# Two tiles gathered ahead, one sweep of four dense tiles, and a subtraction on GpSimd, in a hybrid attention and expert-retrieval layer

## The reference

```python
q = (xb @ w_q).reshape(nb, PEER_HEADS, 2, PEER_KEY_DIM // 2)
s1 = jnp.einsum('nhd,hkd->nhk', q[:, :, 0], keys1).astype(jnp.float32)
s2 = jnp.einsum('nhd,hkd->nhk', q[:, :, 1], keys2).astype(jnp.float32)
v1, i1 = lax.top_k(s1, PEER_TOPK)
v2, i2 = lax.top_k(s2, PEER_TOPK)
...
sc, sel = lax.top_k(cand, PEER_TOPK)
idx = jnp.take_along_axis(cidx, sel, axis=-1)
g = jax.nn.softmax(sc, axis=-1)
h = jnp.einsum('nd,nhkd->nhk', xb, u[idx]).astype(jnp.float32)
a = (jax.nn.gelu(h) * g).astype(xb.dtype)
return jnp.einsum('nhk,nhkd->nd', a, v[idx])
```

## Time and profile before

| | us |
|---|---|
| median of 3 runs | 4570.38 (4570.34 to 4610.2) |
| the profiled execution, its own time | 4569.48 |
| its span | 4567.7 |
| stages ahead of the experts | 0 to 2378 |
| experts, from the first dense matmuls to the last | 2403 to 4535 |
| TensorE busy in the span | 4049.8 (89%) |
| VectorE busy in the span | 2861.7 (63%) |
| GpSimd busy in the span | 979.8 (21%) |

### The profile page before, as it was taken

The page is one execution under the profiler, slowest core; times in us unless marked ns, Lnnn a source line. Parts: engine busy times, 40 slices in busy tenths (PEclk is TensorE's granted clock), DMA queues, the critical chain, the costliest instruction groups (busy, mean ns, idle before and its releaser), DMA issues. The chain is left out here.

```text
span 4567.7 us, 60721 instructions
## 1 busy us (share of the span) xinstructions
PE 4049.8 (89%) x19923; PEld 3409.7 (75%) x19923; DVE 2861.7 (63%) x5530; ACT 1447.8 (32%) x2567; POOL 979.8 (21%) x811
## 2 busy tenths in 40 slices
PE   6999798978878756878559999999999999999996
PEld 5788566734456655777548999999999999999996
DVE  4300354311122098888858888888888888888886
ACT  3111233311112113544443333333333333333333
POOL 0000000000000000000004444444444444444441
PEclk9999899789989777888779999999999999999998
DMA  4322421120040100122129999999999999999995
GB/s 142 116 87 79 117 70 42 41 110 28 19 166 0 42 3 11 78 106 124 78 116 378 341 340 340 339 340 339 340 339 340 339 340 339 339 339 341 336 340 212
DMA packets 387884, 905.89 MB, mean 198 GB/s; under 512 B 41664, under 2 KB 185024, under 8 KB 386496
## 3 DMA queue, kind: packets, MB, share of 16 engines
q1 hardware_dynamic: 257696, 491.80, 30.1%
q0 software_dynamic: 110656, 403.62, 25.1%
q10 hardware_dynamic: 19440, 9.44, 0.7%
HBM read 815.62 MB, written 90.18 MB: 198 GB/s over the span
## 5 line engine op out<-in xcount | busy, mean ns | idle before, releaser
L1968 POOL DMA_INDIRECT exp_gu<-in_peer_u_rows,exp_gidx x384 | 487.0, 1268 | 1372.7 <-DMA exp_ggate<-s_ggate 828.9
L2099 PE MATMUL exp_h<-exp_xh,exp_uh 128*128 128x384 f32 x2048 | 688.1, 336 | 47.5 <-DVE exp_ul L2020 47.5
L2101 PE MATMUL exp_h<-exp_xh,exp_ul 128*128 128x384 f32 x2048 | 688.4, 336 | 0.0
L2100 PE MATMUL exp_h<-exp_xl,exp_uh 128*128 128x384 f32 x2048 | 687.1, 335 | 0.0
L2112 PE MATMUL exp_y<-exp_vh,exp_al 128*128 128x512 f32 x1536 | 602.7, 392 | 0.0
L1974 POOL DMA_INDIRECT exp_gv<-in_peer_v,exp_gidx x384 | 473.0, 1232 | 602.4 <-DVE H L2035 520.0
L2111 PE MATMUL exp_y<-exp_vl,exp_ah 128*128 128x512 f32 x1536 | 602.1, 392 | 0.0
L2110 PE MATMUL exp_y<-exp_vh,exp_ah 128*128 128x512 f32 x1536 | 597.2, 389 | 0.0
L1987 ACT ACTIVATE exp_gel<-exp_h 128x384 f32<-128x384 f32 x256 | 126.0, 492 | 1372.7 <-PE exp_h L2101 1372.7
L2035 DVE SCALAR_TENSOR_TENSOR H<-exp_gv,exp_coef,H 128x1024 f32<-128x1024 f32 x384 | 470.6, 1281 | 10.0 <-issue 0.4
L2025 DVE CUSTOM_DVE_ANT_0 exp_gu<-exp_gu,exp_xg 128x1024 f32<-128x1024 f32 x384 | 449.6, 1222 | 0.0
(11 more groups left out here) (293 smaller groups left out, 5982.8 us busy)
## 6 DMA issues: line engine op xcount, KB each, us to landing
exp_u<-in_peer_u SPq DMA_DIRECT2D x256, 512.0 KB, 5.9
exp_v<-in_peer_v SPq DMA_DIRECT2D x256, 512.0 KB, 6.2
exp_w<-s_w SPq DMA_DIRECT2D x256, 192.0 KB, 6.4
...
exp_gu<-in_peer_u_rows,exp_gidx POOLq DMA_INDIRECT x384, 6.3
```

Source lines behind the costliest of these rows:

```text
L1968: pool.indirect_dma_start(out=gu[i % 2][t][:, :], out_offset=None, in_=I["peer_u_rows"], in_offset=bass.IndirectOffsetOnAxis(ap=gidx[:, t, ...
L2099: pe.matmul(hp[s][:, 0:TC], uh[s][:, c, :], xh[k][:, c, :], start=(c == 0), stop=False)
L2100: pe.matmul(hp[s][:, 0:TC], uh[s][:, c, :], xl[k][:, c, :], start=False, stop=False)
L2101: last = pe.matmul(hp[s][:, 0:TC], ul[s][:, c, :], xh[k][:, c, :], start=False, stop=(c == KD - 1))
```

## The change

Tiles 0 and 1 (NE = 2) go through project, diff, window, merge, memory and retrieve alone first; their lists stay in SBUF. The other seven tiles go through the same phases after them. Meanwhile GpSimd fetches the expert rows of the two early tiles (`fetch`), one `u` row per token, tile and list entry (256 units) and then one `v` row, into a ring of slots, and VectorE takes 256 `dot`s and 256 `axpy`s at written places between the phase's own instructions: 140 dots in project, 84 in diff, 32 in window; 24 axpys in window, 124 in merge, 108 in memory. The ring is the seven late tiles of `H` itself, which project reads first and merge reads again from DRAM; in merge and memory it has slots of its own. All loops over tiles are written out. Retrieve of the late tiles makes three gathered and four dense tiles (before: three and six), and `right` has its two last dimensions exchanged.

Experts is one sweep over 128 blocks with four dense tiles (512 columns). h has one PSUM bank, six banks hold the sums of three tiles, and the eighth bank, `spare`, takes the fourth tile's two halves in turn, which VectorE adds to `H` in every block (`add_half`). The three gathered tiles get one list entry per block. vl is subtracted by GpSimd, behind the six gathers of the next block's rows. Of the diff, the helpers, the build and the experts:

```diff
+def fetch(pool, K, table, ring, came, used, units):
+    for j, u in enumerate(units):
+        if j >= len(ring):
+            pool.wait_ge(used, j - len(ring) + 1)
+        pool.indirect_dma_start(out=ring[j % len(ring)], out_offset=None, in_=table,
+                                in_offset=bass.IndirectOffsetOnAxis(ap=K["gidx"][:, u % NE, u // NE:u // NE + 1], axis=0))\
+            .then_inc(came[j % len(ring)], 16)
+def dot(dve, K, ring, came, used, units, j):
+    u, row = units[j], ring[j % len(ring)]
+    dve.wait_ge(came[j % len(ring)], 16 * (j // len(ring) + 1))
+    dve.tensor_tensor_reduce(out=row, in0=row, in1=K["xg"][:, u % NE, :], scale=1.0, scalar=0.0, op0=ALU.mult, op1=ALU.add,
+                             accum_out=K["dots"][:, u % NE, u // NE:u // NE + 1]).then_inc(used, 1)
+def axpy(dve, K, ring, came, used, units, j):
+    u, row = units[j], ring[j % len(ring)]
+    if u % NE == 0:
+        dve.drain()
+    dve.wait_ge(came[j % len(ring)], 16 * (j // len(ring) + 1))
+    dve.scalar_tensor_tensor(out=K["H"][:, u % NE, :], in0=row, scalar=K["dots"][:, u % NE, u // NE:u // NE + 1],
+                             in1=K["H"][:, u % NE, :], op0=ALU.mult, op1=ALU.add).then_inc(used, 1)
...
+DOTS = (140, 84, 32)
+AXPYS = (24, 124, 108)
+MERGE_SLOTS, MEMORY_SLOTS = 7, 3
...
+        dots, axpys = spans(DOTS), spans(AXPYS)
+        early, late = (0, NE), (NE, NT - NE)
...
+            K["ring"] = []
+            phase_project(nc, sem, K, I, S, *early)
+            release()
             with ExitStack() as scope:
-                for name, shape in kept.items():
-                    K[name] = scope.enter_context(nc.sbuf_tensor(name, shape, F32))
-                for phase in phases:
-                    phase(nc, sem, K, I, S)
-            if held:
-                nc.all_engine_barrier()
-                nc.clear_and_free_semaphores(held)
-                nc.all_engine_barrier()
-                held.clear()
+                mixers(scope, 0, NE)
+                phase_diff(nc, sem, K, I, S, *early)
+                phase_window(nc, sem, K, I, S, *early)
+                phase_merge(nc, sem, K, I, S, *early)
+            release()
+            phase_memory(nc, sem, K, I, S, *early)
+            phase_retrieve(nc, sem, K, I, S, *early, NE)
+            release()
+
+            K["ring"] = [K["H"][:, t, :] for t in range(NE, NT)]
+            phase_project(nc, sem, K, I, S, *late, dots[0])
+            release()
+            with ExitStack() as scope:
+                mixers(scope, 1, NT - NE)
+                phase_diff(nc, sem, K, I, S, *late, dots[1])
+                phase_window(nc, sem, K, I, S, *late, dots[2], axpys[0])
+                phase_merge(nc, sem, K, I, S, *late, axpys[1], MERGE_SLOTS)
+            release()
+            phase_memory(nc, sem, K, I, S, *late, axpys[2], MEMORY_SLOTS)
+            release()
+        phase_retrieve(nc, sem, K, I, S, *late, NG)
+        release()
+        phase_experts(nc, sem, K, I, S)
+        phase_final(nc, sem, K, I, S)
...
                                 last = pe.matmul(kp[2 * r + n // 4][:, (n % 4) * P:(n % 4 + 1) * P], left[r][:, n, :],
-                                                 right[r][:, :, n], start=True, stop=True)
+                                                 right[r][:, n, :], start=True, stop=True)
...
-SWEEPS = 2
-SD = ND // SWEEPS
-TC = SD * P
-NY = 2 * SD
-NQ = SWEEPS * NKEY
+TC = ND * P
+NY = 2 * (ND - 1)
+FIRST_G, FIRST_D = NE, NE + NG
...
-                pool.wait_ge(lists_in, 32)
-                pool.wait_ge(xg_ready, NG)
-                for i in range(NKEY):
+                def up(i):
...
+                def low_v(q):
+                    pool.wait_ge(vh_ready, q + 1)
+                    pool.tensor_tensor(vl[q % 2][:, :], v[q % 2][:, :], vh[q % 2][:, :], ALU.subtract).then_inc(vl_ready, 1)
+
+                pool.wait_ge(lists_in, 32)
+                pool.wait_ge(xg_ready, NG)
+                up(0)
+                for i in range(1, NKEY):
+                    up(i)
+                    down(i - 1)
+                    low_v(i - 1)
+                down(NKEY - 1)
+                low_v(NKEY - 1)
...
+                def add_half(q, half):
+                    dve.wait_ge(half_ready, q * 2 + half + 1)
+                    dst = H[:, NT - 1, half * CW:(half + 1) * CW]
+                    dve.tensor_tensor(dst, dst, spare[:, :], ALU.add).then_inc(half_added, 1)
...
+                def step(q, s, turn, turn_before, further=True, first=False):
 
                     dve.drain()
                     dve.wait_ge(w_in[s], 16 * (turn + 1))
                     dve.wait_ge(h_taken, q + 1)
                     dve.tensor_tensor(prod[:, :], gel[:, :], w[s][:, :], ALU.mult).then_inc(p_ready, 1)
-                    dve.wait_ge(vh_ready, q + 1)
-                    dve.tensor_tensor(vl[s][:, :], v[s][:, :], vh[s][:, :], ALU.subtract).then_inc(vl_ready, 1)
                     dve.wait_ge(ah_ready, q + 1)
                     dve.tensor_tensor(al[s][:, :], prod[:, :], ah[s][:, :], ALU.subtract).then_inc(al_ready, 1)
+                    if not first:
+                        add_half(q - 1, 1)
                     if further:
                         low_u(q + 2, s)
-
-                def pair(q, i, x, turn_q, turn_i, further=True, between=None):
-
-                    step(q, 0, turn_q, further)
-                    if between is not None:
-                        add_up(between)
-                    dot(i, x, turn_i)
-                    step(q + 1, 1, turn_q, further)
-                    axpy(i, x, turn_i)
+                    dot(s, turn, 0)
+                    dot(s, turn, 1)
+                    add_half(q, 0)
+                    dot(s, turn, 2)
+                    if not first:
+                        axpy(q - 1, 1 - s, turn_before)
...
+                def product(y, s, t, half, opens, closes):
+
+                    rows, cols = slice(t * P, (t + 1) * P), slice(half * CW, (half + 1) * CW)
+                    pe.matmul(y[:, :], ah[s][:, rows], vh[s][:, cols], start=opens, stop=False)
+                    pe.matmul(y[:, :], ah[s][:, rows], vl[s][:, cols], start=False, stop=False)
+                    return pe.matmul(y[:, :], al[s][:, rows], vh[s][:, cols], start=False, stop=closes)
 
                 def output(q, s, opens=False, closes=False):
                     pe.wait_ge(vl_ready, q + 1)
                     pe.wait_ge(al_ready, q + 1)
+                    if not opens:
+                        pe.wait_ge(half_added, q * 2)
+                    product(spare, s, ND - 1, 0, True, True).then_inc(half_ready, 1)
                     for x in range(NY):
-                        rows, cols = slice(x // 2 * P, (x // 2 + 1) * P), slice(x % 2 * CW, (x % 2 + 1) * CW)
-                        y = yp[x][:, :]
-                        pe.matmul(y, ah[s][:, rows], vh[s][:, cols], start=opens, stop=False)
-                        pe.matmul(y, ah[s][:, rows], vl[s][:, cols], start=False, stop=False)
-                        last = pe.matmul(y, al[s][:, rows], vh[s][:, cols], start=False, stop=closes)
-                    last.then_inc(block_done, 1)
+                        product(yp[x], s, x // 2, x % 2, opens, closes)
+                    pe.wait_ge(half_added, q * 2 + 1)
+                    product(spare, s, ND - 1, 1, True, True).then_inc(half_ready, 1)
+                    pe.sem_inc(block_done, 1)
...
+                with pe.Fori(1, NKEY // 2) as i:
+                    hidden(i * 2, 0)
+                    output(i * 2 - 1, 1)
+                    hidden(i * 2 + 1, 1)
+                    output(i * 2, 0)
+                output(NKEY - 1, 1, closes=True)
```

More of the change, by code:

```diff
@@ new lines, in _ @@
+                high_w(1, 1)
+                for k in range(max(0, n - 4), n - 2):
+                    store_turned(k)
+                for g_ in range(n, total + 2):
+                    c, t = g_ // n, g_ % n
+                    for half in range(2):
+                        if c < CHUNKS - 1 and HIGH_AT[n][half] == t:
+                            high_w(c + 1, half)
+                    if ROPED <= c < ROPED + PLAIN:
+                        plain_rows(g_)
+                    if g_ - 2 < ROPED * n:
+                        store_turned(g_ - 2)
+                    elif g_ - 2 >= (ROPED + PLAIN) * n:
+                        store_turned(g_ - 2 - PLAIN * n)
@@ L363, in project @@
+                        pe.matmul(z[:, 0:width], xh[:, k, at], high, start=(k == 0), stop=False)
+                        pe.matmul(z[:, 0:width], xh[:, k, at], low, start=False, stop=False)
+                        last = pe.matmul(z[:, 0:width], xl[:, k, at], high, start=False, stop=(k == KD - 1))
                     last.then_inc(z_ready, 1)
                 turn_x(0)
-                pe.wait_ge(wl_ready, 2)
-                for t in range(NT):
-                    if t < NT - 1:
-                        turn_x(t + 1)
-                    pe.wait_ge(xl_ready, t + 1)
```

(38 more changed lines are left out.)

1666 lines of the change are left out of this document (864 added, 802 removed).

## The result

The changed kernel takes 4554.38 us in the median of eleven runs (4544.2 to 4562.56); the kernel before, in the eleven runs made beside it, 4602.33 (4565.89 to 4610.2). The ratio is 0.9916, interval [0.9888, 0.9944]: a gain of 0.8%, where 4360 us, 4.6%, was forecast. Of the eleven runs of the kernel before, four lie between 4566 and 4570 and seven between 4601 and 4610; the forecast was built on one of the four, against which the gain is 0.3%. The profiled execution of the changed kernel is its fastest run, 4544.2, with a span of 4542.2 us.

A forecast was written before the change was run, and what follows sets the result against it. TensorE alone was taken to bound the experts, 8.33 us a block. 4569.48 − 350 (experts) + 135 (stages ahead) + 7 (barriers) = 4361, given as 4360; own range 4270 to 4460, with rivals 4190 to 4500.

The forecast's parts named there:

- About 1.8 of 2.5 us ... is added to VectorE: Experts: engines take turns, so about 1.8 us of GpSimd's 2.5 us subtraction lengthens VectorE's block, 11.96 to 13.8 us.
- I take 0.4 of it, 12 a tile, −47: Retrieve: the new layout of right speeds matmuls, 29 us a dense tile; 0.4 kept, 47 us saved over four tiles.
- The exposed rows: Late stages: of 614 us of early tiles' dots and axpys on VectorE, 158 us lengthen the stages.
- my own bound, 96: Late diff stage: 84 dots, 96 us, don't fit VectorE's idle pieces; exposed between 0 and 96, 60 taken.
- VectorE's sum of a block: Experts: VectorE's work per block with vl gone, summed by instruction starts, 11.96 us before any loss to GpSimd.
- The slow rival: Experts: subtraction takes 4.8 us, all taken from VectorE; block 16.75 us, total 4737; chance 0.10.
- the point where the change stops paying: Experts: break-even at 15.4 us a block, a loss of 3.5 us a block to GpSimd.
- the low rival (no turns): Experts: VectorE stays at 11.96, GpSimd's 12.5 us or the DMA bounds the block; total 4195; chance 0.22.
- Rival 3: Late stages don't hide the early tiles' rows: 350 of 614 us exposed instead of 158; total 4550; chance 0.12.
- that dot kept its 1.23: Experts, for no turns: a VectorE dot kept its length while GpSimd's gather issue beside it stretched from 0.94 to 1.68.

The follow-up runs named there:

- the fill: Changed kernel with GpSimd filling vl with zeros (memset, no read) instead of subtracting, same place in its queue: 4196.47 us in two runs.
- the copy: Changed kernel with GpSimd copying v into vl (one operand read) instead of subtracting, at the same place: 4378.78 us in two runs.
- the move in the queue: Changed kernel with GpSimd's subtraction of vl put ahead of its three gathers of v rows instead of behind them: 4467.9 us, ratio 0.9754.
- the kernel before with this one part: Kernel before with only vl's subtraction moved from VectorE to GpSimd, between its gathers: 4875.18 us, ratio 1.0619.
- the dots better placed: Changed kernel with vl back on VectorE and 54 of diff's 84 dots moved to project (30) and window (24): 4176.08 us, ratio 0.9106.

## Why the prediction was wrong

The forecast was 4360 and the time 4554, 194 us more. The way was right: TensorE is no longer the bound, VectorE is, and what GpSimd's subtraction does to VectorE decides. Three terms were too small or did not come.

- **"About 1.8 of 2.5 us ... is added to VectorE" failed.** 2.75 is added. The rest was meant to lie in VectorE's wait for ah or beside the additions that read PSUM; the rows show the subtraction starting 0.49 us after that wait is over, and al then ends 0.57 us after it. VectorE itself sets this place: its first dot of a block frees the buffer that GpSimd waits for (3511.65), the six gathers are issued without another wait, and the subtraction stands behind them (3520.34), so it meets al in 120 of 128 blocks. The block is 14.7 and not 13.8: 0.9 × 128 = 115 us. That the two engines take turns is shown by the fill (nothing lost), the copy (1.40 for 1.05), the move in the queue and the kernel before with this one part. "SBUF — State Buffer", section "Who interferes with whom", of the Trainium skill says that a VectorE instruction with two SBUF inputs contends with a GpSimd instruction that reads SBUF; these runs agree, with VectorE the loser for 2.14 to 2.75 us and GpSimd for 0.86. On who loses, that the first to start keeps the port, they agree only in part: the dot that began 0.23 us ahead of the subtraction was left whole, but al, whose record begins 0.49 ahead, was not.
- **"I take 0.4 of it, 12 a tile, −47" failed** by 40 us: I priced the matmuls' faster operand, named VectorE as the next bound, and did not price what the edit does to VectorE's own instruction, which now reads with a step. The write of `right` is longer by 0.57 us a batch, as much as VectorE had waited for TensorE, and the gain is 0.11 a batch, 7 us by the rows and 5 by the times.
- **The exposed rows were 193 us and not 158**: diff 97 for 60, memory 61 for 26, project 18 for 12, window 12 for 53, merge 6 for 7. That the sum missed by 35 only is luck, since window's miss stands against those of diff and memory. Diff reached the upper end of my own bound, 96, but not by the mechanism of that bound, dots that VectorE couldn't hide: 39 us are TensorE's longer waits for the softmax rows, 40 its slower matmuls at the lower clock, which no term had, and 12 the longer pause ahead of window.

115 + 40 + 35 = 190; the forecast was missed by 194 in the median, and by 184 in the profiled run that the rows are from. Right in size were VectorE's sum of a block, 11.96 for 11.94, the subtraction, 2.5 for 2.37, and the exposed rows of merge, 7 for 6. The slow rival named the right mechanism, all of the subtraction taken from VectorE, with 4.8 us where 2.37 was measured, and a loss of 3.5 us as the point where the change stops paying; with 2.75 it stayed on the near side. Two rivals come near a measured time by chance. The run with the fill is at 4196, where the low rival (no turns) had 4195, but its block is 11.9 and not 12.5, and the two other terms above make up for that. Rival 3 had 4550 for the changed kernel, but from 350 us of exposed rows, and 193 were measured.

My argument "that dot kept its 1.23" for the other way was read from an instruction that only issues a gather. It said nothing of one that reads a tile, as the forecast itself noted; the range should have gone up to the whole subtraction and beyond, 4500 and more, for its likeliest case.

The change as a whole hides two things in one number: without the subtraction on GpSimd the same rebuild gains 7.9%, and with the dots better placed 8.9%.
